# Gate products of a decoder layer's mixer with high and low weights side by side, and some low parts subtracted on GpSimd instead of VectorE

## The reference

```python
h = modulate(rms_norm(x, g_ffn1), sh1, sc1)
x = x + 0.5 * ga1 * swiglu(h, w_gate1, w_up1, w_down1)        # 1024 -> 2816 -> 1024
h = modulate(rms_norm(x, g_mix), sh2, sc2)
(q_n, k_c, v_c, k_s, v_s, k_w, v_w, gate_n, q_f, k_f, v_f, f_logit,
 gm_nsa, gm_fox) = split(h @ w_in)       # gate_n: 24 columns, f_logit: 8 columns
# ... sigmoid(gate_n) weighs three branches of 8 heads, log_sigmoid(f_logit + b) is summed for 8 heads ...
x = x + ga2 * (sigmoid(gm_nsa) * (o_nsa @ w_up_nsa) + sigmoid(gm_fox) * (o_fox @ w_up_fox)) @ w_o
h = modulate(rms_norm(x, g_ffn2), sh3, sc3)
x = x + 0.5 * ga3 * swiglu(h, w_gate2, w_up2, w_down2)
out = rms_norm(x, g_final)
```

## Time and profile before

| | |
|---|---|
| median of three runs | 2234.31 us |
| the profiled execution | 2234.3 us |
| its span, first to last instruction | 2232.6 us |
| granted TensorE clock, mean | 0.996 of 2.4 GHz |
| busy: PE / DVE / ACT / POOL | 2202.2 / 1559.5 / 1071.6 / 903.2 us |
| share of PE in the chain that ended last | 82% |

### The profile page before, as it was taken

How to read it: one execution, slowest core, us unless ns; L and a number is a source line. 1 busy time by engine, 2 the same in 40 slices (tenths; PEclk the granted TensorE clock), 3 DMA queues, 4 the chain that set the end, 5 groups by cost and what they waited for, 6 DMA issues and landing times.

```text
span 2232.6 us, 29463 instructions
## 1 busy us (share of the span) xinstructions
PE 2202.2 (99%) x10472; PEld 1814.6 (81%) x10472; DVE 1559.5 (70%) x2116; ACT 1071.6 (48%) x2028; POOL 903.2 (40%) x782
## 2 busy tenths in 40 slices
PE   7999999999999999999999999999999999999998
PEld 6888888888887888888787887888778888888887
DVE  7976767578878757732899998578785454547765
ACT  5533333333454553344899898425443333333344
POOL 0044555400122655544557656447205555530013
PEclk9999999999999999999999999999999999999999
DMA  7156565374561533444814065323223222347454
GB/s 281 73 194 221 210 216 202 137 295 165 188 224 50 162 125 137 152 166 141 226 53 119 15 161 152 120 95 142 104 87 126 89 106 103 109 162 262 148 177 160
DMA packets 152033, 338.01 MB, mean 151 GB/s; under 512 B 14224, under 2 KB 36880, under 8 KB 151888
## 3 DMA queue, kind: packets, MB, share of 16 engines
q1 hardware_dynamic: 150624, 333.57, 44.3%
q10 hardware_dynamic: 1264, 2.56, 0.5%
HBM read 247.28 MB, written 86.64 MB: 150 GB/s over the span
## 4 chain that ended last, share of the span: by engine, by line
PE 82%; DVE 11%; ACT 3%; issue 2%; DMA 1%; POOL 1%; SPq 0%; DVEq 0%; ACTq 0%; POOLq 0%
PE ps L3184 11%; PE ps L3185 11%; PE ps L3186 11%; PE ps L3332 6%; PE ps L3330 6%; PE ps L3331 6%; PE ps L3411 4%; PE ps L3413 4%; PE ps L3412 4%; PE ps L3538 3%; PE ps L3563 2%; PE ps L3564 2%; PE ps L3523 2%; PE ps L3142 2%; PE ps L3144 2%
## 5 line engine op out<-in xcount | busy, mean ns | idle before, releaser
L3184 PE MATMUL ps<-r_main,r_z 128*128 128x512 f32 x1232 | 482.0, 391 | 6.1 <-DVE r_main L2212 3.4
L1964 POOL TENSOR_TENSOR r_z<-f_main,r_z 128x512 fp32r<-128x512 f32 x213 | 304.6, 1432 | 446.6 <-ACT r_z L1231 446.6
L3185 PE MATMUL ps<-r_main,r_z 128*128 128x512 f32 x1232 | 480.3, 390 | 0.0
L3186 PE MATMUL ps<-r_main,r_z 128*128 128x512 f32 x1232 | 480.3, 390 | 0.0
L1231 ACT CAST r_z<-f_main 128x512 fp32r<-128x512 f32 x254 | 155.8, 621 | 346.7 <-PE ps L3186 277.5
L3184 PEld LDWEIGHTS ps<-r_main,r_z 128*128 128x128 f32 x1232 | 231.9, 188 | 60.2 <-DVE r_main L2212 4.4
L3186 PEld LDWEIGHTS ps<-r_main,r_z 128*128 128x128 f32 x1232 | 231.8, 188 | 48.2
L3185 PEld LDWEIGHTS ps<-r_main,r_z 128*128 128x128 f32 x1232 | 231.8, 188 | 47.6 <-issue 0.2
L3330 PE MATMUL ps<-r_main 128*128 128x512 f32 x604 | 235.8, 390 | 0.0
L3332 PE MATMUL ps<-r_main 128*128 128x512 f32 x604 | 235.0, 389 | 0.0
L3331 PE MATMUL ps<-r_main 128*128 128x512 f32 x604 | 235.0, 389 | 0.0
(11 more groups left out here) (385 smaller groups left out, 4497.7 us busy)
## 6 DMA issues: line engine op xcount, KB each, us to landing
act_d<-f_main SPq DMA_DIRECT2D x154, 256.0 KB, 2.0
f_main<-act_d SPq DMA_DIRECT2D x70, 512.0 KB, 4.9
f_main<-in_ada SPq DMA_DIRECT2D x56, 512.0 KB, 5.2
f_main<-in_wg SPq DMA_DIRECT2D x20, 1024.0 KB, 5.0
f_main<-in_wu SPq DMA_DIRECT2D x20, 1024.0 KB, 5.0
f_w<-in_wo SPq DMA_DIRECT2D x40, 512.0 KB, 4.0
f_main<-in_wmix SPq DMA_DIRECT2D x18, 1024.0 KB, 5.4
f_e<-in_we SPq DMA_DIRECT2D x10, 1024.0 KB, 5.6
```

Of the source, the lines that this page charges most:

```text
L1964: pool.tensor_tensor(prod_lo_t[slot], source_of(g), prod_hi_t[slot].bitcast(F32), ALU.subtract).then_inc(s["wl"], 1)
L3184: pe.matmul(out, wh, hi, start=start, stop=False, skip_group_check=True)
L3185: pe.matmul(out, wh, lo, start=False, stop=False, skip_group_check=True)
L3186: return pe.matmul(out, wl, hi, start=False, stop=stop, skip_group_check=True)
```

## The change

1. Gate weights: only 64 of the 128 columns are used. For each feature tile the 64 high columns and, beside them, the 64 low columns are kept in one 128-column tile (`gate_w`). Two matmuls, with the high and with the low part of x, take the place of three; rows 0 to 63 of the result are the products with the high weights, rows 64 to 127 those with the low ones. ScalarE copies rows 64 to 127 to SBUF (`gate_lows`), VectorE adds rows 0 to 63 (`gate_sum`), then the sigmoid is applied to rows 32 to 63 in place.
2. x low parts of combinations 6 and 4 go from VectorE to GpSimd, in all three parts of the layer (`X_POOL`): in the feed-forward parts behind the weight low parts 14 and 21, in the mixer behind 2 and 5. They count `s_added`; `x_split` waits for the semaphore that fits.
3. The weight low parts 8 to 27 of both feed-forward parts go from VectorE to GpSimd.

```diff
+X_POOL = (6, 4)
+X_AFTER = {14: 6, 21: 4}
...
+        def x_split(engine, k, q, i):
+
+            if q in X_POOL:
+                engine.wait_ge(s_added, 3 + 8 * k + 4 * X_POOL.index(q) + i + 1)
+            else:
+                engine.wait_ge(nsem["hl"], HL[k] + (20 + i + 1 if q == 5 else x_count(q, i, k)))
...
+            def gate_lows(h):
+
+                act.copy(gate_f[0:HD, halves(h)], ps_at(plain_bank[GATES_T][h])[HD:P]).then_inc(q_["gsg"], 1)
...
-                act.activation(gate_f[:, halves(0)], ps_at(plain_bank[GATES_T][0]), ACT.Sigmoid).then_inc(q_["gsg"], 1)
+                gate_lows(0)
...
-                act.activation(gate_f[:, halves(1)], ps_at(plain_bank[GATES_T][1]), ACT.Sigmoid).then_inc(q_["gsg"], 1)
+                gate_lows(1)
...
-                act.wait_ge(q_["gsg"], 2)
+                act.wait_ge(q_["gsg"], 4)
                 for h in range(NH):
-                    act.copy(gate_f[0:8, halves(h)], ps_at(plain_bank[GATES_T][h])[0:8]).then_inc(q_["gsg"], 1)
+                    act.activation(gate_f[32:HD, halves(h)], gate_f[32:HD, halves(h)], ACT.Sigmoid).then_inc(q_["gsg"], 1)
...
+            def x_low(k, q):
+
+                for i in range(4):
+                    pool.wait_ge(nsem["hh"], HH[k] + x_count(q, i, k))
+                    pool.tensor_tensor(x_lo[k][q][:, i], chunk(q, i), x_hi[k][q][:, i].bitcast(F32), ALU.subtract).then_inc(s_added, 1)
...
-            pool.wait_ge(fsem[0]["wl"], fbase[0]["wl"] + SECOND + 6)
-            for g in range(SECOND + 6, N_PROD):
+            pool.wait_ge(fsem[0]["wl"], fbase[0]["wl"] + PRELUDE)
+            for g in range(PRELUDE, N_PROD):
                 weight_low(0, g)
+                if g in X_AFTER:
+                    x_low(0, X_AFTER[g])
...
             for g in range(M_PROD):
                 mix_weight_low(g)
+                if g in (2, 5):
+                    x_low(1, {2: 6, 5: 4}[g])
...
-            for g in range(PRELUDE):
+            for g in range(N_PROD):
                 weight_low(1, g)
-            pool.wait_ge(fsem[1]["wl"], fbase[1]["wl"] + SECOND + 6)
-            for g in range(SECOND + 6, N_PROD):
-                weight_low(1, g)
+                if g in X_AFTER:
+                    x_low(2, X_AFTER[g])
...
                 for i in range(4):
                     t2(k, i)
                 weight_sum(f, 1, UP, 1)
-                weight_low(f, 13)
-                weight_low(f, 14)
-                for i in range(4):
-                    x_low(k, 6, i)
                 weight_sum(f, 1, UP, 2)
-                weight_low(f, 15)
-                weight_low(f, 16)
                 x_low(k, 5, 0)
...
                 for i in range(4):
                     t4(k, i)
-                x_low(k, 4, 0)
-                x_low(k, 4, 1)
                 plain_taken(f, 2)
-                x_low(k, 4, 2)
                 plain_taken(f, 3)
-                x_low(k, 4, 3)
...
+            def gate_sum(h):
+
+                dve.wait_ge(q_["gsg"], 2 * h + 1)
+                total = gate_f[0:HD, halves(h)]
+                dve.tensor_tensor(total, total, ps_at(plain_bank[GATES_T][h])[0:HD], ALU.add).then_inc(q_["gsg"], 1)
...
-                for q in (6, 5):
-                    for i in range(4):
-                        x_low(1, q, i)
+                for i in range(4):
+                    x_low(1, 5, i)
+                gate_sum(0)
                 mix_taken(2)
+                gate_sum(1)
                 mix_sum(0, 4)
-                for i in range(5):
-                    if i < 4:
-                        t4(1, i)
-                    if i > 0:
-                        x_low(1, 4, i - 1)
+                for i in range(4):
+                    t4(1, i)
                 mix_taken(4)
...
+            def plain_product(e, h, part, i):
+
+                out, q = ps_at(plain_bank[e][h]), ((1, 2), (8, 3))[h][part]
+                first, last = (part, i) == (0, 0), (part, i) == (1, 3)
+                hi, lo = x_hi[1][q][:, i], x_lo[1][q][:, i]
+                if e == GATES_T:
+                    pe.matmul(out, gate_w[:, 4 * part + i], hi, start=first, stop=False)
+                    return pe.matmul(out, gate_w[:, 4 * part + i], lo, start=False, stop=last)
+                return product3(out, plain_hi[e][part][:, i], plain_lo[e][part][:, i], hi, lo, first, last)
```

## The result

The changed kernel takes 2254.84 us (2253.80 to 2255.15), the kernel before, run beside it, 2234.35 us; a fourth run of the changed kernel, 2335.43 us at a mean granted clock of 0.903, was in a slower state and isn't counted. The ratio is 1.0092 with a 95% interval of 1.0074 to 1.0110: 20.5 us slower. The forecast was 2249.4 us with a range to 2258.0, so the sign and the range held. The forecast sum of losses was 15.1 us, 5 us short. The profiled execution of the changed kernel took 2254.5 us with a span of 2252.7, so the spans differ by 20.1 us, and that is what has to be found in the traces.

A forecast was written before the change was run, and what follows sets the result against it. TensorE is busy 99% of the span, beside a VectorE with almost no slack that takes turns with GpSimd. Losses of 6.2 + 4.1 + 4.8 = 15.1 us on 2234.3 gave 2249.4 us, range 2231.0 to 2258.0.

The forecast's parts named there:

- forecast sum of losses: Losses of first feed-forward, mixer and second feed-forward, 6.2 + 4.1 + 4.8 = 15.1 us.
- The alternation: GpSimd and VectorE steps with both inputs in SBUF take turns: 1.10 us for GpSimd, 0.60 for VectorE.
- the walk through the turns: Following VectorE's and GpSimd's lists turn by turn in both feed-forwards and the mixer; losses 6.2, 4.1 and 4.8 us.
- the statistic: Mixer's second statistic, already waiting 0.27 us for VectorE; 0.9 us of saved gate matmuls turn into waiting there.
- product 15: First feed-forward: starts at 97.2 after its cast and low part, TensorE due at 94.3; loss 2.9 us.
- the transposes: Gates' transposes behind the mixer's product 6, at 725.98 before; that product now ends at 730.1, loss 4.1 us.
- (a): Rival: all moved steps are hidden, at all three places; 2231.6 or 2228.9 us; chance 0.14.
- (b): Rival: partly hidden, losses 2.7 to 7 us, 2234 to 2238.6, no measurable change; chance 0.16.
- (c): Rival: backlog spreads into steady pairs, more seeds 2 us late in feed-forwards and mixer; 2259.4 us; chance 0.07.
- (d): Rival: the gates don't lose their matmuls; called not possible by the code, two calls where three stood.
- the seed of product 24: Copied by ScalarE behind a cast hanging on lows 22 to 25; first feed-forward 128.1 instead of 121.9, loss 6.2 us.
- the saved 2.7 us: Gates' 16 fewer matmuls save 3.6 us, 0.9 becomes waiting; 2.7 us left, mixer's first product at 702.7 instead of 705.4.

The follow-up runs named there:

- e5_extra: Kernel before plus 28 extra 128x512 GpSimd subtractions in the first feed-forward part, on a tile nobody reads; 2255.49 us, ratio 1.0092.
- e2_moves: Changed kernel with the gates back in three products, so only the moves of low parts to GpSimd remain; 2254.56 us, ratio 1.0094.
- e8_two: Changed kernel, but GpSimd computes only 32 of 512 columns of the weight low parts of products 22 and 23; 2251.89 us, ratio 1.0076.
- e3_weights: Changed kernel with only the 20 weight low parts of each feed-forward part moved, x low parts and gates as before; 2244.28 us, ratio 1.0048.
- e9_late: e1_gates with VectorE's two gate additions behind the low parts of combination 4 and ScalarE's second gate copy later; 2235.11 us, ratio 1.0005.
- e1_gates: Changed kernel with every low part back on its old engine, so only the gates in two products remain; 2234.62 us, ratio 1.0002.
- e10_reverse: e9_late with the seven weight low parts of the mixer's first unit moved from GpSimd to VectorE; 2232.68 us, ratio 0.9992.
- e12_behind: e10_reverse with the two gate additions behind, not ahead of, the addition that product 6 waits for; 2231.99 us, ratio 0.9989.

## Why the prediction was right, and where it was short

**The alternation held.** The step on which the forecast rested, 1.10 us into VectorE's list for 0.60 out of it, is what the rows of both kernels show, and e5_extra shows that such turns alone cost time, with nothing else changed; the walk through the turns was close for as long as it was made. The first differences ended at 79.6 (forecast 79.5), the statistic waited 1.17 (0.27 + 0.9), and product 15 started at 97.72 (97.2) for GpSimd's low part, in TensorE's rows of the changed kernel below, which answer to the earlier trace rows. In the mixer the transposes start at 739.64, less the 9.75 of the part before it 729.9 (730.1), and the loss there was 3.91 (4.1).

```profile
97.72 0.50 PE L3200 MATMUL ps<-r_main,r_z 128*128 128x512 f32 x1 [1.66 <-POOL r_z L1987]
...
683.43 1.10 PE L3153 MATMUL ps<-f_z,ones_f 128*128 128x512 f32 x2 [1.17 <-DVE f_z L2181]
...
739.64 1.03 PE L3410 MATMUL ps<-ident_f,f_z 128*128 128x128 f32 x8
```

**The rivals.** (a) and (b) fell with the count that spoke against them: VectorE didn't run ahead. What was said for (b) was no argument for it: 1 us less at each of six stalls leaves 17.8 - 6 = 11.8 us before the 2.7, which is 2243.4 and inside the forecast's own range. (c), more seeds late in the steady pairs, didn't happen: behind the late seed of the first feed-forward part TensorE has one new wait to the end of the part, of 0.30. The point of (d) stands, 10456 matmuls are 16 fewer.

**The mis-sized term is the seed of product 24**, in both feed-forward parts. The forecast stopped its walk at combination 4 and let ScalarE's seed follow "behind a cast that hangs on the lows 22 to 25", with product 24 at 128.1 and 126.7. It left out that VectorE's four activation sums stand in between, that they wait for GpSimd's last low part, and that two of GpSimd's steps are queued beside them. In the first part they took 4.77 instead of 2.74, and the seed was ready at 130.16. In e2_moves, where TensorE waits for it, product 24 starts at 130.29, 2.2 us behind the forecast. In the changed kernel's own profile TensorE comes later than the seed, at 131.23 and without a wait; why stands below. In the second part product 24 starts at 1691.51, which is 128.8 on the first part's clock with the 12.91 us of lateness taken off, 2.1 later than forecast. TensorE's row, which answers to the earlier trace rows:

```profile
1691.51 0.47 PE L3200 MATMUL ps<-r_main,r_z 128*128 128x512 f32 x1 [1.08 <-ACT ps L1261]
```

That is 4.3 us of the 5.0 by which the sum was short. e8_two confirms the cause for the second part (2.2 us back). For the first it does so only with the prologue's 1.41 us taken off (1.9 back).

**The rest of the first part.** 9.75 against 6.2 + 2.2 leaves 1.3 us. 0.3 is a wait in the down products, and 0.9 is product 24, which starts at 131.23 in the changed kernel's profile and not at 130.29. There TensorE's clock was granted at 0.50 from 118 to 122 us, in e2_moves's, with nearly the same waits ahead of it, at 1.00 (TensorE's windows: us, busy, clock, DMA, GB/s; the changed kernel, with its row of product 24, then e2_moves).

```profile
118.00:122.00 4.00, 4.00 (x17) 0.50 0.34 127
...
131.23 0.39 PE L3200 MATMUL ps<-r_main,r_z 128*128 128x512 f32 x1
```

```profile
118.00:122.00 4.00, 4.00 (x28) 1.00 0.41 155
...
130.29 0.47 PE L3190 MATMUL ps<-r_main,r_z 128*128 128x512 f32 x1 [1.12 <-ACT ps L1261]
```

But e2_moves has the same span of 2252.7 and the same median within 0.3 us, and its loss in this part is 9.18, 0.6 less, so the lower clock cost 0.9 at product 24 at most, of the 20: a TensorE at full speed waits for the seed instead. Between the mixer's first unit and the second feed-forward part 0.75 us come back. They come back in e3_weights, e9_late and others too (0.4 to 0.7); I haven't traced where.

**Part 1 was sized wrongly in kind.** The forecast took the saved 2.7 us as a gain inside the mixer's 4.1. By e1_gates they are worth next to nothing (0.41 in the mixer's stretch, none in the median) while VectorE's list is the bound, and by e2_moves the mixer loses 3.96 without them, the same as with them. The net came out right because the walk followed VectorE's and GpSimd's lists, and TensorE's early arrival fell out of it.

## What to carry to other kernels

Before work is moved from VectorE to GpSimd, look for a place in the trace where both have work with inputs in SBUF: if two such steps take turns, a moved step makes VectorE's list longer whenever it costs VectorE more than it saves there (here 1.10 for 0.60), and moving GpSimd's steps back to a tight VectorE made it shorter here. Fills on GpSimd, which only write, cost VectorE nothing here. Walk the lists to the last hand-over of the stretch, through every operation between the last moved step and the instruction that TensorE waits for, and not only to the moved steps' own readers. Before a difference of 1 or 2 us in one stretch is put down to an edit, look whether it stands in the trace already ahead of the first edited instruction.

## What the runs showed of the hardware that I had not expected

**What a GpSimd step costs VectorE differs with what the step is.** Per step: 1.09 us for a subtraction of two tiles, 0.84 for one that reads the same tile twice, 0.41 for a copy, nothing for a fill. Among those that read, the longer step holds longer, as said above.

**The granted clock falls in one execution and not in another behind the same wait.** e9_late, e10_reverse and e12_behind do the same work in the first feed-forward part. Behind the waits of the prologue, TensorE's windows of the three show it at 0.53 in one stretch, 0.50 in another, and at 1.00 throughout, in that order; 1.0 is the level of 2.4 GHz and 0.5 that of 1.2. The wait ahead of 35 us is 1.58 us in all three. The one ahead of 27 us is 2.18 in e9_late and 1.79 and 1.87 in the others.

```profile
27.00:30.00 3.00, 2.93 (x7) 0.53 1.03 391
35.00:41.00 6.00, 4.42 (x20) 1.00 0.55 218
```

```profile
27.00:30.00 3.00, 2.75 (x12) 1.00 1.04 393
35.00:41.00 6.00, 5.78 (x14) 0.50 0.55 220
```

```profile
27.00:30.00 3.00, 2.71 (x12) 1.00 1.03 389
35.00:41.00 6.00, 5.75 (x25) 1.00 0.54 214
```

Their first stretch is 1.77, 1.36 and -0.11 us off the kernel before. Of this 1.35 us are there at 36.64 in e9_late (35.29 before), and 1.16 at combination 4 in e10_reverse (111.74 against 110.58), the stretches right behind the low clock. So 1.2 to 1.4 us of a difference between two single profiles of this kernel can go with the clock. In such a case the medians and the place where the lateness begins have to decide.
